# A PEER layer's value stage: one token block by gathered rows on VectorE, three blocks summed in PSUM over all keys

## The reference

```python
scores = jnp.einsum('thpc,hpnc->thpn', q, sub_keys)        # two sets of 128 keys in each head
s_top, i_top = lax.top_k(scores, PEER_TOPK)
cand = (s_top[:, :, 0, :, None] + s_top[:, :, 1, None, :]).reshape(T, PEER_HEADS, 256)
best, pos = lax.top_k(cand, PEER_TOPK)
expert_idx = jnp.take_along_axis(cand_idx, pos, axis=-1)   # i * 128 + j
gates = jax.nn.softmax(best, axis=-1)
u, vv = expert_u[i_blk], expert_v[i_blk]                   # 128 picks for each token
act = jax.nn.gelu(jnp.einsum('td,tkd->tk', h_blk, u), approximate=False)
out = jnp.einsum('tk,tkd->td', act * g_blk, vv)
x = layer_norm(ALPHA * x + out, ln2_gain, ln2_bias)
```

## Time and profile before

| | us |
|---|---|
| median of 3 runs (lowest, highest) | 2237.18 (2232.27, 2237.53) |
| the profiled execution | 2237.41 |
| its span in the trace | 2235.7 |
| TensorE busy | 2198.1 |
| VectorE busy | 1066.0 |
| ScalarE busy | 642.3 |
| GpSimd busy | 873.6 |

### The profile page before, as it was taken

How to read it: one execution, slowest core, us unless ns; L and a number is a source line. 1 busy time by engine, 2 the same in 40 slices (tenths; PEclk the granted TensorE clock), 3 DMA queues, 4 the chain that set the end, 5 groups by cost and what they waited for, 6 DMA issues and landing times.

```text
span 2235.7 us, 30141 instructions
## 1 busy us (share of the span) xinstructions
PE 2198.1 (98%) x10588; PEld 1761.3 (79%) x10588; DVE 1066.0 (48%) x2397; ACT 642.3 (29%) x936; POOL 873.6 (39%) x369
## 2 busy tenths in 40 slices
PE   7999999999989999999999999999999999999998
PEld 5786556788778888878888888888888888888887
DVE  3001224111411999965555544223366656566666
ACT  4523213322143333333333333322212121211211
POOL 6432001444153444434444444453344443534441
PEclk9997569999999999999999999999999999999999
DMA  5321000233332333446666666764455554645551
GB/s 175 102 76 47 1 10 24 90 99 99 123 114 88 121 130 138 141 146 189 188 188 190 190 188 188 240 231 155 159 198 192 183 206 170 215 178 207 189 186 75
DMA packets 146354, 325.65 MB, mean 146 GB/s; under 512 B 9185, under 2 KB 74849, under 8 KB 137970
## 3 DMA queue, kind: packets, MB, share of 16 engines
q1 hardware_dynamic: 51264, 184.57, 25.0%
q10 hardware_dynamic: 95026, 140.23, 18.2%
HBM read 255.56 MB, written 69.21 MB: 145 GB/s over the span
## 4 chain that ended last, share of the span: by engine, by line
PE 86%; DVE 12%; issue 0%; ACT 0%; DMA 0%; SPq 0%; DVEq 0%; ACTq 0%
PE bank L354 25%; PE bank L356 24%; PE bank L355 24%; PE bank L615 4%; PE bank L447 2%; PE bank L469 2%; DVE cand L1144 1%; PE bank L459 1%; DVE cand L1142 1%; PE bank L484 1%; DVE ijg L1145 1%; PE bank L492 1%; PE bank L450 1%; DVE top_i L1119 1%; DVE top_i L1110 1%; DVE score L1113 1%
## 5 line engine op out<-in xcount | busy, mean ns | idle before, releaser
L333 POOL TENSOR_TENSOR w_lo<-stage,w_hi 128x1024 fp32r<-128x1024 f32 x348 | 868.1, 2512 | 1319.0 <-ACT w_hi L666 1319.0
L354 PE MATMUL bank<-x_hi,w_lo 128*128 128x512 f32 x1376 | 545.7, 397 | 8.5 <-DVE x_lo L973 5.6
L356 PE MATMUL bank<-x_hi,w_hi 128*128 128x512 f32 x1376 | 538.2, 391 | 0.0
L355 PE MATMUL bank<-x_lo,w_hi 128*128 128x512 f32 x1376 | 537.3, 390 | 0.0
L666 ACT ACTIVATE w_hi<-stage 128x1024 fp32r<-128x1024 f32 x348 | 350.9, 1043 | 577.3 <-PE bank L356 561.8
L354 PE MATMUL bank<-w_hi,wt_lo 128*128 128x512 f32 x1024 | 398.3, 389 | 0.0
L355 PE MATMUL bank<-w_lo,wt_hi 128*128 128x512 f32 x1024 | 398.3, 389 | 0.0
L356 PE MATMUL bank<-w_hi,wt_hi 128*128 128x512 f32 x1024 | 398.3, 389 | 0.0
L1200 DVE TENSOR_TENSOR acc<-acc,bank 128x512 f32<-128x512 f32 x256 | 174.9, 684 | 336.5 <-PE bank L356 336.5
L354 PEld LDWEIGHTS bank<-x_hi,w_lo 128*128 128x128 f32 x1376 | 259.6, 189 | 61.8 <-DVE x_lo L973 6.5
L356 PEld LDWEIGHTS bank<-x_hi,w_hi 128*128 128x128 f32 x1376 | 259.5, 189 | 55.6
(11 more groups left out here) (204 smaller groups left out, 1848.2 us busy)
## 6 DMA issues: line engine op xcount, KB each, us to landing
stage<-in_expert_uT SPq DMA_DIRECT2D x128, 512.0 KB, 3.5
stage<-in_expert_v SPq DMA_DIRECT2D x128, 512.0 KB, 3.5
stage<-in_mix_stream SPq DMA_DIRECT2D x84, 512.0 KB, 3.4
gates<-gate_scratch ACTq DMA_DIRECT2D x32, 1024.0 KB, 4.8
act<-activation_scratch ACTq DMA_DIRECT2D x32, 1024.0 KB, 6.9
activation_scratch<-act_out_a ACTq DMA_DIRECT2D x64, 256.0 KB, 2.5
activation_scratch<-act_out_b ACTq DMA_DIRECT2D x64, 256.0 KB, 2.4
gate_scratch<-gstage_a ACTq DMA_DIRECT2D x8, 2048.0 KB, 11.1
```

The source lines that it names most:

```text
L333: nc.gpsimd.tensor_tensor(w_lo[:, slot, 0:width], stage[:, slot % STAGE, 0:width], w_hi[:, slot, 0:width], ALU.subtract).then_inc(split_do ...
L354: mm(dst, l_lo, r_hi, start=first, stop=False)
L355: mm(dst, l_hi, r_lo, start=False, stop=False)
L356: return mm(dst, l_hi, r_hi, start=False, stop=last)
```

## The change

- The V tiles no longer alternate with U tiles: all 128 U tiles come first, then all 128 V tiles.
- Token block 0 leaves the dense products of gates and values. Its 128 picks are done one after the other: GpSimd issues an indirect transfer of one value row of 1024 for each token (`gather_row`, 128 rows of 4 KB, 4 buffers `gat`), and VectorE adds it, times the pick's weight, to `acc0` (`add_pick`). The pick's activation comes by another indirect transfer of one number for each token (`gather_act`), 128 of them too. The U tiles still do all 512 tokens.
- Blocks 1 to 3 accumulate over all 128 V tiles in six PSUM banks (2 to 7). A V tile is 18 matmuls, and `acc` and `add_out` go. The U tiles keep two banks where they had four.
- ScalarE makes `wt_hi` (`round_weight`); VectorE keeps the product and `wt_lo`, over 384 tokens, in five buffers. GpSimd keeps every `w_lo`.
- `groups_by` and `picks_by` spread the 96 groups of gates over U tiles 50 to 97, and the 128 picks over V tiles 10 to 116 (86 tiles with one pick, 21 with two). Block 0's layer norm is put at V tiles 121 to 123; the others stay at the end.

```diff
+FIRST_PICK = 10
+LAST_PICK = 116
+def picks_by(v):
+    return max(0, min(NPICK, (v - FIRST_PICK + 1) * NPICK // (LAST_PICK - FIRST_PICK + 1)))
...
 # GpSimd
+            def gather_act(k):
+                nc.gpsimd.indirect_dma_start(out=weight[:, k:k + 1], out_offset=None, in_=acts,
+                                             in_offset=bass.IndirectOffsetOnAxis(ap=aidx[:, k:k + 1], axis=0)
+                                             ).then_inc(act_got[k // CHUNK_PICKS], 16)
+            def gather_row(k):
+                if k >= GATHER:
+                    pool.wait_ge(picked, k - GATHER + 1)
+                nc.gpsimd.indirect_dma_start(out=gat[:, k % GATHER, :], out_offset=None, in_=rows,
+                                             in_offset=bass.IndirectOffsetOnAxis(ap=eidx[:, k:k + 1], axis=0)
+                                             ).then_inc(gathered[k % GATHER], 16)
+            for tile in range(2 * NKEY):
+                n, v = first_expert + tile, tile - NKEY
                 split_low(n, n % RING, QW)
+                if v == FIRST_PICK - 6:
+                    pool.wait_ge(eidx_ready, 1)
+                    for parity in range(2):
+                        pool.wait_ge(act_written[parity], 16 * NKEY // 2)
+                while acts_due < min(NPICK, 4 * (v - FIRST_PICK + 7), picks_by(v - 4) + 2 * CHUNK_PICKS):
+                    gather_act(acts_due)
+                    acts_due += 1
+                while rows_due < picks_by(v - 4):
+                    gather_row(rows_due)
+                    rows_due += 1
...
 # TensorE
+            for v in range(NKEY - TAIL_TILES):
+                pe.wait_ge(split_done, first_value + v + 1)
+                pe.wait_ge(wt_done, v + 1)
+                for b in range(1, TB):
+                    for half in range(2):
+                        ins = value_part(v, b, half)
+                ins.then_inc(quarter_used, 1)
...
 # ScalarE
+            def round_weight(v):
+                sc.wait_ge(wt_mul, v + 1)
+                if v >= WT:
+                    sc.wait_ge(quarter_used, first_value + v - WT + 1)
+                act_f(wt_hi[:, v % WT, :], act[:, v // UNIT % 2, v % UNIT, :], ACT.Copy).then_inc(wt_hi_done, 1)
+            for v in range(1, NKEY):
+                round_weight(v)
+                if v + 3 < NKEY:
+                    ahead(first_value + v + 3)
+                if v % UNIT == 0 and v // UNIT + 1 < NUNIT:
+                    sc.wait_ge(wt_done, v)
+                    load_unit(v // UNIT + 1)
...
 # VectorE
+            weigh(0)
+            for w in range(NKEY):
+                if w + 1 < NKEY:
+                    weigh(w + 1)
+                weight_low(w)
...
+                for k in range(picks_by(w - 1), picks_by(w)):
+                    if k % CHUNK_PICKS == 0:
+                        weigh_picks(k // CHUNK_PICKS)
+                    add_pick(k)
```

More of the change, by code:

```diff
@@ L126, in build @@
+        gates = at("gates", [P, 2, NGB, UNIT, GB], F32, Q + 20)
+        act = at("act", [P, 2, UNIT, ND], F32, Q + 32)
+        wt_hi = at("wt_hi", [P, WT, ND], F32R, Q + 60)
+        wt_lo = at("wt_lo", [P, WT, ND], F32R, Q + 67.5)
+        ln_g2 = at("ln_g2", [P, D], F32, Q + 44)
+        ln_b2 = at("ln_b2", [P, D], F32, Q + 48)
         E = Q + 80
@@ L265, in _ @@
                     m += 1
-            for k in range(gate_tiles):
+            for k in range(NKEY):
                 load(first_expert + k, expert_uT[k])
[L269 to L286, removed]
+            for k in range(NKEY):
+                load(first_value + k, expert_v[k])
             for t in range(TB):
                 sp.wait_ge(y_ready, t + 1)
-                sp.dma_start(out[t * P:(t + 1) * P, :], acc[:, t, :]).then_inc(y_out, 16)
+                sp.dma_start(out[t * P:(t + 1) * P, :], acc0[:] if t == 0 else x1[:, t, :]).then_inc(y_out, 16)
             sp.wait_ge(y_out, 16 * TB)
@@ new lines, in _, with value_part @@
+            for t in range(TB):
+                key_scores(t)
+            pe.wait_ge(sc_evac, 4 * TB)
+            for tile in range(NKEY):
+                if tile in TURN_AT:
+                    turn_picks(TURN_AT[tile])
+                score_tile(tile)
+                for g in range(groups_by(tile - 1), groups_by(tile)):
+                    gate_group(g)
+            def value_part(v, b, half):
+                n = first_value + v
+                s, w = n % RING, v % WT
+                r, c = slice((b - 1) * P, b * P), slice(half * 512, half * 512 + 512)
+                return mm3(bank[2 * b + half][:], wt_hi[:, w, r], wt_lo[:, w, r], w_hi[:, s, c], w_lo[:, s, c],
+                           v == 0, v == NKEY - 1)
@@ L648, in _ @@
+            for b in range(1, TB):
+                for half in range(2):
+                    for v in range(NKEY - TAIL_TILES, NKEY):
+                        ins = value_part(v, b, half)
+                    ins.then_inc(ffn_done, 1)
         @block.scalar
@@ L923, in _ @@
+            for t in range(NKEY):
+                if t in EXP_AT:
+                    exp_gates(EXP_AT[t])
+                if t in TURN_AT:
+                    evac_picks(TURN_AT[t])
+                gelu_tile(t)
+                ahead(first_expert + t + 4)
+                store_tile(t)
+                for g in range(groups_by(t - 1), groups_by(t)):
+                    evac_group(g)
+                if t == last_group_tile + 2:
                     for half in range(2):
@@ L961, in _ @@
+            for t in range(1, TB):
+                normalize(t)
         @block.vector
@@ L1124, in _, with first_level @@
+            def first_level(t):
+                dve.wait_ge(sc_evac, 4 * t + 4)
+                step(top16(top_v, top_i, score[t], HP))
                 v.tensor_copy(top_if[:], top_i[:])
@@ new lines, in _ @@
+            for t in range(1, TB):
+                for half in range(2):
+                    c = slice(half * 512, half * 512 + 512)
+                    dve.wait_ge(ffn_done, 2 * (t - 1) + half + 1)
+                    ins = v.scalar_tensor_tensor(out=x1[:, t, c], in0=x1[:, t, c], scalar=ALPHA, in1=bank[2 * t + half][:],
+                                                 op0=ALU.mult, op1=ALU.add)
+                step(ins)
+                norm_stats(x1[:, t, :], t).then_inc(ln2_var, 1)
+                norm_apply(x1[:, t, :], t, ln_g2, ln_b2, ln2_var, ln2_sqrt, y_ready)
```

565 lines of the change are left out of this document (252 added, 313 removed).

## The result

The changed kernel took 2930.63 us in the median of 4 runs (2929.43 to 2931.68), the kernel before 2237.03 us on the same chips. The ratio is 1.3107, 95% interval 1.3084 to 1.3129. The profiled execution's span is 2927.7 us.

The account below looks back on a forecast made before the run. A tile-to-tile latency loop in the V stage was taken to bound the kernel: 1509 + 70 + 1258 + 51 + 8.4 = 2896 us of span, plus 1.7 us, gave 2898 us; range 2600 to 3150.

Parts of the forecast that it names:

- TensorE's saving and the start of the value stage: On TensorE: 174 us from fewer matmuls and 22.4 us from fewer gate groups saved; V stage begins at 1509 us.
- Start of the ring: At the V stage's beginning: first activation fetches and low parts delay the end of pick 0 to 70 us after it.
- low part: GpSimd's step over 128x1024 for a V tile: 2.38 us, 2.45 with the hand-over.
- The ring: V stage, loop through VectorE, ScalarE and GpSimd: each tile costs the whole latency, 11.87 us, 1258 us for 106 rounds.
- an issue: GpSimd's issue of one indirect transfer: estimated at 1.1 us, 2.09 of them in a round.
- a row lands: V stage: landing of a 512 KB value row, 3.5 us from the issue's end, bounds 2.4 and 4.8.
- TensorE's clock: V stage: granted clock 0.50, a tile 8.2 us, free under the round; 5 us added for getting back to full clock.
- The tail: After TensorE's last matmul: one add, a layer norm and the store, 8.4 us.
- cheap issues: Rival, V stage: issues of 0.33 us and rows landing in 2.4 us, round 9.2 us, time 2583 us; chance 0.10.
- dear ones: Rival, V stage: issues near 2.4 us or rows landing late, up to 3370 us; chance 0.15 for more than 3080.
- The rival on the other side: V stage: throughput decides, VectorE and GpSimd only exclude each other, 5.0 us a tile, 2170 us; chance 0.04.

Follow-up runs that it names:

- e1: Changed kernel, but GpSimd issues the rows for tile w's picks behind the low part of tile w+3, not w+4; 2398.02 us.
- e4: Changed kernel, but ScalarE copies the high part of tile v+4, not v+3, behind the weight's high part of tile v; 2386.65 us.
- e10: Changed kernel, but VectorE makes the product of tile w+2, not w+1, ahead of the picks of w; 2384.92 us.
- e8: Changed kernel, rows behind tile w+4 as before, with only the V tiles' low parts moved from GpSimd to VectorE; 2092.02 us.
- e6: As e2, but without the 128 activation fetches (a pick's weight is its gate squared); 2156.49 us.
- e2: Changed kernel, but GpSimd issues the rows for tile w's picks behind the low part of tile w+2, not w+4; 2250.69 us.
- e5: As e2, but the low parts of all 128 V tiles move from GpSimd to VectorE; 2087.09 us.

## Why the prediction held, step by step

- **TensorE's saving and the start of the value stage**: put at 1509 us; the first V matmul starts at 1496.6. Of the 12 us, 6 are pauses between 715 and 1400 us that the prediction kept and that are gone: TensorE was idle for 5.6 + 1.2 us there, and is now for 0.7. The other 6 were not traced.
- **Start of the ring**: the first pick was to end 70 us later; it ended 78.8 us later (1575.4). Between the low parts of two tiles with four fetches lie 7.44 us, where 2.4 + 4 x 1.1 = 6.8 were assumed; over eight tiles that is 5 of the 9 us.
- **The ring**: 106 rounds took 1296 us (1575.4 to 2871.7), not 1258: 12.2 against 11.87 us each. That it exists, and that it bounds, e1, e4, e10 and e8 show. The terms: an issue is 0.94 to 0.97 us, with 0.30 ahead of the next, so 1.27 for the activation fetch where 1.1 stood; a row lands a median of 4.8 us from its issue's start, where 1.1 + 3.5 = 4.6 stood; low part 2.51 for 2.45; the pick 1.20 for 1.34, `wt_hi` 0.43 for 0.52. They make the ring 38 us longer than put down, with errors both ways in them. The total is off by only 32 us because the stages around the ring took part of that back: -12 for the earlier start, +9 for the late first pick, -3 behind the ring. The mechanism was right; that the total came so near is partly luck.
- **TensorE's clock**: the mean granted clock in the value stage was 0.73 to 0.77 and not 0.50. It changed between its two levels within a tile: around 2012 us the first matmuls of a tile started 0.43 us apart, its last 0.23. That costs nothing there, as said. Coming back to full clock cost 1.7 us and not 5: the last eleven tiles took 2919.4 - 2872.8 = 46.6 us against 44.9.
- **The tail**: 8.3 us, where 8.4 stood.
- **Two slips that change nothing**: VectorE's 436 of 806 us leave it 46%, not half or more. And product, `wt_hi`, `w_hi`, low part and pick sum to 6.03 us in the prediction's own terms (9.53 - 3.5), not 5.76, which only strengthens the argument it stands in.
- **The rivals**: cheap issues are refuted by the 0.94 us, dear ones too. The rival on the other side, that VectorE and GpSimd exclude each other at 5.0 us a tile, was a true mechanism waiting behind the ring, as the stretched picks of e6 and the longer issues of e2 show once more tiles share the latency. Its price was too low for the kernel with all its fetches (2170 us; e2 is at 2251), since the 5.0 us counted none of GpSimd's 2.09 issues a tile, nor that VectorE's work stretches them. By the Trainium skill (SBUF — State Buffer, SBUF: two separate sides) the port pair that VectorE and GpSimd share is an exclusive lock, and whichever starts first keeps it for its whole instruction. The trace agrees for the low parts in that one of the two waits until the other is done (picks end 1.08 and 1.09 us behind the low part), but not that the first to start goes first: the pick of 1898.37 did not, the one of 1677.16 did.
- The Trainium skill's figure for a transfer from GpSimd (3.2 us for 512 KB, DMA: Bandwidth & Descriptors, Anatomy of one DMA — SWDGE (gpsimd) path) is under what was measured: a row landed 4.8 us from its issue's start, 4.8 - 0.94 = 3.9 us from its end.

## What to carry to other kernels

Buffers do not make a pipeline. Follow one item through the queues of all engines and note at each wait which item of the engine ahead it stands behind: if the path comes back to the first engine n items later, an item costs the path's whole latency over n, however many buffers there are. Here n was 1; moving one constant by one in any of three queues saved 533 to 546 us, and taking the cheap step that hung on the ring (the low part) off the engine that issues transfers saved 839. Once the latency is shared, count next what the busiest engine needs for an item, with its instructions as long as they are beside the other engine's: GpSimd's low part and stretched issues held e2 at 5.9 us a tile, where the lengths of the changed kernel gave 5.1.

## What the runs showed of the hardware

- An indirect transfer of 128 rows occupies GpSimd for 0.94 us with rows of 4 KB and 0.97 with 4 bytes a row (medians of 128 in the changed kernel), and the next begins 0.30 us later.
- VectorE's two-input work stretches such an issue as well: median 0.942 us in the changed kernel, 1.726 in e5, up to 2.99 there. Within e5, from 1560 to 2020 us, the 29 issues with no VectorE instruction beside them took 0.93 to 0.95 us, the 160 with 0.9 us or more of VectorE's work beside them a median of 1.77. In e5 the reverse was not seen: a pick took at most 1.287 us.
- A low part on GpSimd and a two-input instruction on VectorE exclude each other: in e6 a pick took 3.92 us and not 1.28 (1898.37), and a low part 3.04 and not 2.37 (1677.66).

From e5, busy ns as min/median/max:

```profile
L360 POOL DMA_INDIRECT gat<-in_expert_v,eidx x128: 933/1726/2990, 1550.9 to 2016.6; - x128
L1096 DVE SCALAR_TENSOR_TENSOR acc<-gat,weight,acc x128: 1270/1279/1287, 1555.3 to 2026.2; 128x1024 f32<-128x1024 f32 x128
```
